# Moving a cumulative sum from behind the recurrent gates into the steps beside the projections, and a product from VectorE to GpSimd

## The reference, cut to what matters

```python
xa, ga, q, k, v, f_logit, g_a, g_b = jnp.split(proj, offs, axis=-1)
xc = causal_dwconv(xa, conv_a_w[layer], conv_a_b[layer])
hr = rg_lru(xc, w_rg_a[layer], b_rg_a[layer], w_rg_x[layer], b_rg_x[layer], lru_lambda[layer])
y_a = jax.nn.gelu(ga) * hr
y_b = forgetting_attention(q, k, v, f_logit + b_forget[layer])
...
# in rg_lru: r, i = sigmoid(xb @ w_a + b_a), sigmoid(xb @ w_x + b_x), block by block of 80
log_a = -LRU_C * r.astype(jnp.float32) * jax.nn.softplus(-lam.astype(jnp.float32))
a = jnp.exp(log_a)
b_term = jnp.sqrt(-jnp.expm1(2.0 * log_a)) * (i * xc).astype(jnp.float32)
# h[t] = a[t] * h[t-1] + b_term[t]
...
# in forgetting_attention
cum = jnp.cumsum(jax.nn.log_sigmoid(f_logit.astype(jnp.float32)), axis=1).transpose(0, 2, 1)
```

## Time and profile before

| | us |
|---|---|
| median of 3 runs | 3068.13 (3067.24 to 3068.77) |
| profiled execution | 3068.77 |
| its span | 3067.0 |
| PE busy in the span | 2910.6 (95%) |
| DVE busy | 1885.4 (61%) |
| ACT busy | 1567.5 (51%) |
| POOL busy | 365.0 (12%) |

### The profile page before, as it was taken

How to read it: one execution, slowest core, us unless ns; L and a number is a source line. 1 busy time by engine, 2 the same in 40 slices (tenths; PEclk the granted TensorE clock), 3 DMA queues, 4 the chain that set the end, 5 groups by cost and what they waited for, 6 DMA issues and landing times.

```text
span 3067.0 us, 46899 instructions
## 1 busy us (share of the span) xinstructions
PE 2910.6 (95%) x19486; PEld 2677.0 (87%) x19486; DVE 1885.4 (61%) x3088; ACT 1567.5 (51%) x2487; POOL 365.0 (12%) x322
## 2 busy tenths in 40 slices
PE   7999899799989997999889999999999999999998
PEld 7978898699768986789888999999888889989896
DVE  4556554545565555667765589677555556645775
ACT  4444444544444445446554444677555455644663
POOL 0000000000000000100000244688000000000000
PEclk9999999899978998999899999999999999999999
DMA  6544455355424553535426455333555564535453
GB/s 200 186 151 157 148 192 188 110 187 191 153 76 144 197 185 126 178 97 158 145 64 196 165 179 179 138 131 132 192 192 192 193 222 129 174 89 185 152 198 125
DMA packets 304227, 490.49 MB, mean 160 GB/s; under 512 B 10816, under 2 KB 236480, under 8 KB 295312
## 3 DMA queue, kind: packets, MB, share of 16 engines
q1 hardware_dynamic: 302880, 480.09, 47.3%
q0 software_dynamic: 1136, 7.41, 0.7%
HBM read 485.36 MB, written 2.10 MB: 159 GB/s over the span
## 4 chain that ended last, share of the span: by engine, by line
PE 88%; DVE 6%; ACT 4%; issue 1%; POOL 1%; DMA 0%; SPq 0%; DVEq 0%; POOLq 0%; ACTq 0%
PE ps L471 30%; PE ps L440 17%; PE ps L441 16%; PE ps L444 16%; PE ps L895 2%; ACT AR L2211 1%; DVE halves L1141 1%; DVE AR L1193 1%; PE ps L929 1%; ACT XH L2196 1%; POOL st L1026 1%; PE ps L422 1%; PE ps L949 1%; DVE AR L1859 1%; PE ps L642 0%
## 5 line engine op out<-in xcount | busy, mean ns | idle before, releaser
L2182 ACT ACTIVATE halves<-raw 128x1024 fp32r<-128x1024 f32 (+2 forms) x907 | 950.2, 1053 | 970.3 <-PE ps L444 505.2
L1141 DVE TENSOR_TENSOR halves<-raw,halves 128x1024 fp32r<-128x1024 f32 (+2 forms) x858 | 1032.0, 1218 | 404.4 <-ACT halves L2182 401.6
L440 PE MATMUL ps<-XH,halves 128*128 128x256 f32 x3968 | 997.4, 288 | 7.8 <-DVE XL L1165 5.0
L441 PE MATMUL ps<-XL,halves 128*128 128x256 f32 x3968 | 986.8, 286 | 0.0
L440 PEld LDWEIGHTS ps<-XH,halves 128*128 128x128 f32 x3968 | 769.8, 194 | 14.0 <-DVE XL L1165 6.6
L441 PEld LDWEIGHTS ps<-XL,halves 128*128 128x128 f32 x3968 | 770.2, 194 | 1.0
L444 PE MATMUL ps<-XH,halves 128*128 128x256 f32 x3968 | 561.1, 284 | 1.5 <-DVE halves L1141 1.5
L444 PEld LDWEIGHTS ps<-XH,halves 128*128 128x128 f32 x3968 | 515.1, 193 | 2.7 <-DVE halves L1141 2.1
L471 PE MATMUL ps<-halves,R 128*128 128x512 f32 x1872 | 429.2, 391 | 3.6 <-DVE halves L1141 1.9
L471 PEld LDWEIGHTS ps<-halves,R 128*128 128x128 f32 x1872 | 352.5, 189 | 77.6 <-DVE halves L1141 2.3
L471 PE MATMUL ps<-halves,XH 128*128 128x512 f32 x1600 | 405.7, 393 | 13.0 <-ACT halves L2182 7.2
(11 more groups left out here) (338 smaller groups left out, 2537.4 us busy)
## 6 DMA issues: line engine op xcount, KB each, us to landing
raw<-in_w_ffn_in SPq DMA_DIRECT2D x88, 1024.0 KB, 5.1
raw<-in_w_in SPq DMA_DIRECT2D x74, 1024.0 KB, 5.3
raw<-in_uT SPq DMA_DIRECT2D x64, 1024.0 KB, 4.8
raw<-in_peer_v SPq DMA_DIRECT2D x64, 1024.0 KB, 4.9
raw<-in_w_ffn_out SPq DMA_DIRECT2D x44, 1024.0 KB, 4.9
raw<-in_w_up SPq DMA_DIRECT2D x24, 1024.0 KB, 5.4
raw<-in_mlstm_w_in SPq DMA_DIRECT2D x12, 1024.0 KB, 5.3
raw<-in_w_down SPq DMA_DIRECT2D x12, 1024.0 KB, 5.0
```

What stands on the lines that cost most here:

```text
L440: mm(o, hi[:, q, 0:M], xh[:, k0 + q, :], start=first and q == 0, stop=False)
L441: mm(o, hi[:, q, 0:M], xl[:, k0 + q, :], start=False, stop=False)
L1141: te.tensor_tensor(lo, src, hi.bitcast(F32), ALU.subtract).then_inc(k.lo_made, 1)
L2182: act(hi, src, ACT.Copy).then_inc(k.hi_made, 1)
```

## The change

It does three things in `mix3`:

- PE does `small` after the gates of the recurrence in place of before them. DVE's bias add of the logits and ACT's exponential move with it.
- On DVE `cum_rows` isn't run through ahead of q any more, but is the first part of the side `lru`: 10 steps ahead of the old ones. ACT's side gets the exponential and 9 further empty steps in the same place. Both sides are taken four steps at a time in place of two.
- The two products with gelu(ga), 128x1280 each, move from DVE to POOL. Each waits for the scans of its half, and ACT's copy waits for POOL.

```diff
@@ tensor_engine, mix3
         features("m3.ga", 10, X, rx)
-        small("m3", 1, 96, rx)
         pe.wait_ge(*k.dma["rg_in"].need(1))
...
                 filled(("m3.rg", f, i), ins)
+        small("m3", 1, 96, rx)
@@ gpsimd_engine
+    xc, ya = k.ar(0, 10, 256), k.ar(12288, 10, 256)
+    for f in range(0, 10, 5):
+        gp.wait_ge(*s["vec"].need(("m3.h", f + 4)))
+        gp.wait_ge(*k.main.gone(("m3.ga", 8)))
+        nc.gpsimd.tensor_tensor(ya[:, f:f + 5].rearrange("p a b -> p (a b)"),
+                                ya[:, f:f + 5].rearrange("p a b -> p (a b)"),
+                                xc[:, f:f + 5].rearrange("p a b -> p (a b)"), ALU.mult) \
+            .then_inc(*s["pool"].mark(("m3.ya", f)))
@@ vector_engine, mix3
         def lru():
+            yield from cum_rows()
             for f in range(0, 10, 5):
...
             for f in range(0, 10, 5):
-                v.wait_ge(*step.need(("m3.h", f + 4)))
-                v.wait_ge(*main.gone(("m3.ga", 8)))
-                te.tensor_tensor(flat(ya[:, f:f + 5]), flat(ya[:, f:f + 5]), flat(xc[:, f:f + 5]), ALU.mult) \
-                    .then_inc(*s["part"].mark(("m3.ya", f)))
-                yield
-            for f in range(0, 10, 5):
...
-        for _ in cum_rows():
-            pass
-        v.begin(lru(), 2)
+        v.begin(lru(), 4)
@@ scalar_engine, mix3
-        a.wait_ge(*main.gone(("m3", "small")))
-        exp_neg_abs(e_, cum, "m3.e")
         for f in range(0, 10, 2):
...
         def lru():
+            a.wait_ge(*main.gone(("m3", "small")))
+            exp_neg_abs(e_, cum, "m3.e")
+            for _ in range(1 + 6 + 1 + 1 + 1):
+                yield
             for f in range(0, 10, 5):
                 yield
...
             for f in range(0, 10, 5):
-                yield
-            for f in range(0, 10, 5):
-                a.wait_ge(*s["part"].need(("m3.ya", f)))
+                a.wait_ge(*s["pool"].need(("m3.ya", f)))
...
-        a.begin(lru(), 2)
+        a.begin(lru(), 4)
```

More of the change, by code:

```diff
@@ L2685, in mix3 @@
         features(out_of("m3.ga", ya, ACT.Gelu_apprx_tanh), "m3.ga", 10)
-        rw = [k.AR[0:96, 25216 + 256 * i:25472 + 256 * i] for i in range(2)]
-        cum, e_ = rw
-        weights()
-        a.wait_ge(*main.gone(("m3", "small")))
-        exp_neg_abs(e_, cum, "m3.e")
         for f in range(0, 10, 2):
@@ L2699, in mix3 @@
         qT, kT, vv = k.ar(17536, 8, 256), k.ar(19584, 8, 256), k.ar(21632, 2, 1024)
+        rw = [k.AR[0:96, 25216 + 256 * i:25472 + 256 * i] for i in range(2)]
+        cum, e_ = rw
+        weights()
         def flat(z):
```

## The result

| | before | after |
|---|---|---|
| median | 3068.39 us (4 runs) | 3085.97 us (4 runs, 3085.74 to 3090.82) |
| profiled execution, span | 3068.77, 3067.0 | 3086.56, 3084.8 |

The ratio is 1.0057, with a 95% interval from 1.0046 to 1.0069: slower by 17.6 us. The forecast was 3085.0, within 3080 to 3090. The mechanism was as predicted and so was nearly every step up to k3; three terms behind it were mis-sized or missing, and their errors largely cancel.

What follows compares the result with a forecast made beforehand. TensorE was taken as the bound, busy all of the time around the change. Stalls of 14.7 us plus 1.5 of low clock gave 16.2, added to 3068.77: 3085.0 us, forecast as 3085, range 3080 to 3090.

Steps and rivals of the forecast that it cites:

- PE is the bound, nothing can be won: Around the change and 189 us behind it, TensorE never waits and loses no matmul; a gain had chance 0.01.
- 12.2 us of the sum and 2.9 of products ahead of q6's low half: On VectorE, uncovered work delays the low half of q's sixth weight piece: a TensorE stall of 5.6 us.
- The recurrence packed by four steps: After the first stall, side work at four steps per weight piece keeps making VectorE's low halves late, by 0.7 to 2.4 us.
- k1 and k2, 0.8 and 1.3: At the first two weight pieces of k, VectorE's low halves come late: stalls of 0.8 and 1.3 us.
- at 1280 columns that is 3.0, at most 4.6. I take 3.1: Length of each product of gate and recurrence moved to GpSimd, from its subtraction rows: 3.1 us taken.
- The last stall, 3.1, behind POOL's second product: At k's sixth weight piece, VectorE waits for ACT's copy, which waits for GpSimd: TensorE stalls 3.1 us.
- 1.5 us of clock behind the last stall: After k's sixth weight piece, TensorE runs at half clock with nothing behind to take it back: 1.5 us added.
- the slow POOL: Rival: GpSimd's second product takes 4.6 us instead of 3.1 beside VectorE, last stall 4.6, time 3086.5; chance 0.1.
- The lead takes it all: Rival: VectorE's lead of up to two weight pieces, 5.8 us, hides the side work; not slower, 3068; chance 0.05.

## Why the prediction came true, point by point

- **PE is the bound, nothing can be won** (right). No variant of the change beat the kernel before; the best, two steps with the product on DVE, equals it.
- **12.2 us of the sum and 2.9 of products ahead of q6's low half** (right). The sum started 1.4 us after q1's low half was wanted, as in the working, and the stall was 5.4 with its edges for 5.6. The experiments show what the sum costs without its cover: with two steps nothing, run in one piece 11.1.
- **The recurrence packed by four steps** (right). Alone it costs 6.6. k3 lost 2.48 for 2.4 predicted, and its low half was ready 0.65 us earlier than predicted, counted from q1.
- **k1 and k2, 0.8 and 1.3** (0 and 0.28). The halves were ready 0.45 and 0.6 earlier than predicted (counted from q1), but the larger part is PE, which had lost 1.53 at half clock in q7 and wanted them that much later. The prediction said that the clock's loss behind the first stall would be taken out of the next ones, and it was.
- **POOL: "at 1280 columns that is 3.0, at most 4.6. I take 3.1"** (failed, the mis-sized term). Its bounds hold for POOL's own rows, 3.19 and 3.82. But the step priced only POOL's time. A low half of DVE, k4's, took 3.86 in place of 1.2, which stood in no term. By the rule cited from the Trainium skill (GPSIMD Engine Reference, 8. Key points) the two contend where DVE has two inputs, and the trace agrees, with this 3.86 us. I took the median row against it because POOL stood at 2.4 us in most rows. That was misread. Most of these rows stand beside no work of DVE or beside its searches (MAX8, FIND_INDEX8), as the 2.40 us at 1831.54. And where DVE's low half started second, POOL kept its time and DVE paid: POOL took 2.41 us at 1883.38, and the low half at 1883.91 took 2.96. The trace of before shows both directions, on both engines' rows:

```profile
1839.78 2.01 DVE L1141 TENSOR_TENSOR halves<-raw,halves 128x1024 fp32r<-128x1024 f32 x1 [0.88 <-ACT halves L2182]
```

```profile
1837.30 3.40 POOL L1031 TENSOR_TENSOR halves<-raw,halves 128x1024 fp32r<-128x1024 f32 x1 [3.36 <-ACT halves L2182]
```

  POOL, released at 1837.30 in the middle of a DVE product that ends at 1838.44, takes 3.40 and ends at 1840.70; the low half that starts at 1839.78 takes 2.01 and ends 1.1 us after POOL.
- **The last stall, 3.1, behind POOL's second product** (2.05 in size; the chain is half right). The terms of the working give 2654.85 for k6's low half, so 3.0 rather than 3.1. The predicted wait of DVE for ACT's copy doesn't show. ACT's second copy ended at 2655.42 and DVE's first low half of the product at 2655.46, since POOL's product had held it directly. Either way alone leads to the same time, so the hold of that row (4.21 us for 1.45) cost nothing on top. POOL's product ended 2.6 us later than predicted (counted from q1): the scans before it 1.9 later, and 0.7 since its row took 3.82. That the stall is smaller is k5's low clock, which had made PE 2.41 later already.
- **1.5 us of clock behind the last stall** (failed). The clock was full there. It fell behind q6 and k4, where DVE was late anyway; k6's low half was ready at 2658.08 by DVE's chain whatever PE did.

The sum is thus: predicted stalls 14.7, less 0.65 (the chain up to k3), plus 2.66 (k4's low half), plus 0.7 (POOL's second product) gives 17.4, for 17.46 measured up to k6 and 17.54 with k7. That the forecast was off by only 1 us is in part luck: the 3.4 us left out for POOL stand against 0.65 too much and 1.5 of clock that didn't come there.

Of the rivals, the slow POOL was in part true: POOL wasn't slow in itself, but each engine was held by the other, and DVE's side cost more than POOL's. "The lead takes it all" is what happens with two steps, as its text said; the order of the instructions decided against it. Left open is what makes the clock fall: stalls of 2.99 and 5.13 brought a fall, as one of 1.91 did in the earlier trace rows, one of 3.64 (four steps, product on DVE) and one of 1.98 didn't, and one of 2.3 did in one execution and not in another.

## What to carry to other kernels

An engine that is ahead hides added work only as far as the work is spread: look at how much stands between two deliveries, not at the mean load, since the same sum of 12.2 us cost nothing at two steps a piece, 11.1 in one lump, and 14.9 at four steps together with the rest of the recurrence, which is packed as tightly. Before a VectorE operation is moved to GpSimd, look in the trace for VectorE's own rows beside GpSimd's: what is freed on one queue can come back as a held instruction on the same engine. A stall of TensorE of 2 us is to be priced with a low clock that can come behind it: here one of 2.3 us had nothing behind it in one execution and 6.8 us in another.

## What the runs showed of the hardware

- VectorE's operations with two inputs and GpSimd's with two ran one after the other, whole instructions long. DVE's subtraction took 3.86, 3.92 and 3.93 for 1.2 beside a product of POOL; POOL's 1.47 became 4.05 beside a run of four subtractions. With one input, 2.13 became 4.80 beside such a run, but two-input operations of VectorE in its last 2 us took 0.71 and 0.68 as ever. Between a run of scans and a subtraction POOL got its turn at once; in a run of four subtractions it got it only at the end. What decides that isn't settled.
- GpSimd's operation with one input (128x768, 2.13) was slower than that with two (1.47).
- The same kernel with the same wait of 2.3 us had 13.7 us of low clock behind it in one execution and none in the other, and its ten times fall into two groups, with medians 7 us apart.
